# A transformer pair on one core: RMS norms without a scaling step, and pair scores issued ahead of transposes

## The reference, cut to what matters

```python
def rmsnorm(x, g):
    x32 = x.astype(jnp.float32)
    y = x32 * lax.rsqrt(jnp.mean(x32 * x32, axis=-1, keepdims=True) + EPS)
    return (y * g.astype(jnp.float32)).astype(x.dtype)
```

```python
s = einsum('bnqhgd,bnshd->bnhgqs', q, kb) * HEAD_DIM ** -0.5 + bias     # 64-wide heads
s = where(mask, s, -inf)
p = softmax(concatenate([s, sink], axis=-1), axis=-1)[..., :-1]
o = einsum('bnhgqs,bnshd->bnqhgd', p, vb)
return o.reshape(B, S, N_HEADS * HEAD_DIM) @ w_out
```

## Time and profile before

| what | value |
|---|---|
| median of three runs | 2370.95 us |
| profiled execution, its own time | 2369.46 us |
| its span | 2367.7 us |
| TensorE busy | 2346.6 us, 99% |
| VectorE busy | 1437.1 us, 61% |
| ScalarE busy | 1149.5 us, 49% |
| GpSimd busy | 23.9 us, 1% |
| granted TensorE clock, mean | 0.998 |
| HBM traffic | 185 GB/s over the span |

### The profile page before, as it was taken

How to read it: one execution, slowest core, us unless ns; L and a number is a source line. 1 busy time by engine, 2 the same in 40 slices (tenths; PEclk the granted TensorE clock), 3 DMA queues, 4 the chain that set the end, 5 groups by cost and what they waited for, 6 DMA issues and landing times.

```text
span 2367.7 us, 28497 instructions
## 1 busy us (share of the span) xinstructions
PE 2346.6 (99%) x11298; PEld 1963.7 (83%) x11298; DVE 1437.1 (61%) x2039; ACT 1149.5 (49%) x1704; POOL 23.9 (1%) x35
## 2 busy tenths in 40 slices
PE   8999999999999999999999999999999999999998
PEld 7888888888888888888888887788888888888886
DVE  6445565665554454454444566657888888885444
ACT  6445454545444444444444566655544444444442
POOL 1000000000000000000000100000000000000000
PEclk9999999999999999999999999999999999999999
DMA  7666555655666666666666665455666666666564
GB/s 261 187 187 175 156 174 152 186 185 181 195 187 189 193 188 188 193 188 205 191 191 190 209 197 163 131 151 179 188 193 189 189 193 188 189 193 191 192 194 151
DMA packets 226420, 439.25 MB, mean 186 GB/s; under 512 B 13632, under 2 KB 17888, under 8 KB 225904
## 3 DMA queue, kind: packets, MB, share of 16 engines
q1 hardware_dynamic: 224400, 429.51, 60.5%
q0 software_dynamic: 1888, 7.93, 1.1%
HBM read 435.24 MB, written 2.15 MB: 185 GB/s over the span
## 4 chain that ended last, share of the span: by engine, by line
PE 97%; ACT 1%; DVE 1%; issue 0%; DMA 0%; POOL 0%; DVEq 0%; ACTq 0%; POOLq 0%
PE bank L1357 24%; PE bank L1359 24%; PE bank L1358 24%; PE bank L1387 14%; PE bank L1389 7%; PE bank L1399 2%; PE bank L1543 1%; PE bank L1564 1%; PE bank L1442 0%; ACT whi L605 0%; PE bank L1459 0%; PE bank L1540 0%; PE bank L1565 0%; PE bank L1444 0%; ACT JK L597 0%
## 5 line engine op out<-in xcount | busy, mean ns | idle before, releaser
L906 DVE TENSOR_TENSOR wlo<-raw,whi 128x1024 fp32r<-128x1024 f32 (+1 forms) x812 | 988.1, 1218 | 883.3 <-ACT whi L605 882.6
L605 ACT CAST whi<-raw 128x1024 fp32r<-128x1024 f32 (+1 forms) x812 | 847.4, 1044 | 1158.7 <-PE bank L1359 907.0
L1357 PE MATMUL bank<-whi,TT 128*128 128x512 f32 (+1 forms) x1488 | 591.2, 397 | 3.2 <-DVE wlo L906 3.1
L1359 PE MATMUL bank<-whi,TT 128*128 128x512 f32 (+1 forms) x1488 | 578.2, 389 | 0.0
L1358 PE MATMUL bank<-wlo,TT 128*128 128x512 f32 (+1 forms) x1488 | 577.4, 388 | 0.0
L1387 PE MATMUL bank<-TT,whi 128*128 128x512 f32 x1408 | 488.9, 394 | 0.8 <-DVE TT L1147 0.7
L1389 PE MATMUL bank<-TT,wlo 128*128 128x256 f32 x1408 | 390.1, 277 | 0.0
L1357 PEld LDWEIGHTS bank<-whi,TT 128*128 128x128 f32 x1488 | 279.9, 188 | 62.1 <-DVE wlo L906 4.0
L1358 PEld LDWEIGHTS bank<-wlo,TT 128*128 128x128 f32 x1488 | 280.1, 188 | 58.1 <-issue 2.9
L1359 PEld LDWEIGHTS bank<-whi,TT 128*128 128x128 f32 x1488 | 279.6, 188 | 58.1
L1387 PEld LDWEIGHTS bank<-TT,whi 128*128 128x128 f32 x1408 | 264.0, 188 | 62.5 <-issue 1.3
(11 more groups left out here) (211 smaller groups left out, 1586.6 us busy)
## 6 DMA issues: line engine op xcount, KB each, us to landing
raw<-in_ffn_w_up_dram SPq DMA_DIRECT2D x176, 512.0 KB, 3.6
raw<-in_w_in_dram SPq DMA_DIRECT2D x120, 512.0 KB, 3.7
raw<-in_w_gate_dram SPq DMA_DIRECT2D x88, 512.0 KB, 3.7
raw<-in_w_up_dram SPq DMA_DIRECT2D x88, 512.0 KB, 3.7
raw<-in_w_down_dram SPq DMA_DIRECT2D x88, 512.0 KB, 4.7
raw<-in_ffn_w_down_dram SPq DMA_DIRECT2D x88, 512.0 KB, 4.8
raw<-in_swa_w_in_dram SPq DMA_DIRECT2D x48, 512.0 KB, 3.6
raw<-in_w_out_dram SPq DMA_DIRECT2D x32, 512.0 KB, 4.6
```

The source lines that it names most:

```text
L605: eng.copy(whi[:, t % RING, 0:a * n], raw[:, t % RAW, 0:a * n]).then_inc(s_cast, 1)
L906: eng.tensor_tensor(wlo[:, t % RING, 0:a * n], raw[:, t % RAW, 0:a * n], whi[:, t % RING, 0:a * n].bitcast(F32), ALU.subtract).then_inc(s_ ...
L1357: eng.matmul(o, lh[:, ts], hi[:, kk, :], start=start, stop=False)
L1359: mm = eng.matmul(o, ll[:, ts], hi[:, kk, :], start=False, stop=stop)
```

## The change

It has two parts. In the norms, `square` passes scale = width^-0.5 to ScalarE's Square, so each sum is already divided by the width; `SS` has ten columns for a norm instead of eight, filled with EPS by one memset at the start of VectorE's program, and each half (token tile) of a norm owns one more column, which nothing overwrites. `reduce_sum` takes that column in too, and the multiply-add at L1004 goes, with the wait in front of it. ScalarE waits once for the memset. In `side_steps`, wherever a step t has a `pscore`, every `pptr` and `ppcp` of that t is taken out of the list and put back right behind the first `pscore`. By the table of steps this alters four lists: in 511 and 519 the order "ppcp, pptr, pscore" becomes "pscore, ppcp, pptr", and in 512 and 520 "ppcp, psoft, pscore" becomes "psoft, pscore, ppcp". The banks of these steps change with the order.

```diff
@@ side_steps @@
+    for t in range(END):
+        late = [z for z in at[t] if z[0] in ("pptr", "ppcp")]
+        if any(z[0] == "pscore" for z in at[t]):
+            rest = [z for z in at[t] if z not in late]
+            n = rest.index(next(z for z in rest if z[0] == "pscore"))
+            at[t] = rest[:n + 1] + late + rest[n + 1:]
     put(544, "gain", 2)
@@ build @@
-        SS = sb("SS", [P, 9, 8])
+        SS = sb("SS", [P, 9, 10])
@@ square @@
+                n = (SQ[r] - (SQ[r - 1] if r else 0)) // 2
+                col = col // n * (n + 1) + col % n
+                ac.wait_ge(s_eps, 1)
                 if squares[0]:
                     ac.wait_ge(s_sq, squares[0])
                 squares[0] += 1
-                eng.activation(JK[:, 0:src.shape[-1]], src, ACT.Square,
+                eng.activation(JK[:, 0:src.shape[-1]], src, ACT.Square, scale=SQ_WIDTH[r] ** -0.5,
                                accum_out=SS[:, r, col:col + 1]).then_inc(s_sq, 1)
@@ mean_of @@
-                eng.reduce_sum(MEAN[:, r, :], SS[:, r, 0:2 * n].rearrange("p (t n) -> p t n", n=n),
-                               AX).then_inc(s_red, 1)
-                ve.wait_ge(s_red, r + 1)
-                eng.tensor_scalar(MEAN[:, r, :], MEAN[:, r, :], 1.0 / SQ_WIDTH[r], EPS, ALU.mult,
-                                  ALU.add).then_inc(s_mean, 1)
+                eng.reduce_sum(MEAN[:, r, :], SS[:, r, 0:2 * n + 2].rearrange("p (t n) -> p t n", n=n + 1),
+                               AX).then_inc(s_mean, 1)
@@ vector_program @@
+            eng.memset(SS[:, :, :], EPS).then_inc(s_eps, 1)
             first_T(0)
```

More of the change, by code:

```diff
@@ L368, in build @@
         l_lines, l_gf, l_g1, l_g3, l_bt0, l_bt1, l_out = sems("lines gf g1 g3 bt0 bt1 out")
-        s_sq, s_red, s_mean, s_rs, s_rs34, s_mhalf = sems("sq red mean rs rs34 mhalf")
+        s_sq, s_eps, s_mean, s_rs, s_rs34, s_mhalf = sems("sq eps mean rs rs34 mhalf")
         s_pf, s_ang, s_nn, s_sin, s_trig, s_gfn, s_biasmm, s_biasln = sems(
```

## The result

The changed kernel took 2376.72 us in the median of 22 runs (2367.84 to 2378.62), beside 2370.28 us for the kernel before in 22 runs of the same chip (2369.45 to 2371.42). The forecast was 2369.1 us, the range ended at 2371.2, and the median lies 5.5 us above that end.

A forecast was written before the change was run, and what follows sets the result against it. The prediction took TensorE, busy 2346.6 of 2367.7 us, to bound the kernel. The order's 1.27 us plus three norms at 0.19 gave 1.84 less: 2370.95 - 1.84 = 2369.1 us, range 2367.5 to 2371.2.

The forecast's parts named there:

- The order: Steps 511 and 519: TensorE's waits for YL move onto the last two transposes, gaining 0.64 and 0.63, together 1.27 us.
- The norms: Multiply-add dropped from nine norms: three touch the chain and gain 0.19 us each; the other six were taken as nothing.
- norms 6 and 8: Transposes of X after one norm, bare end of program at the other: 0.19 us less each without the multiply-add.
- norm 0: Chain from L1004 through the power and ScalarE back to TensorE: 0.19 us earlier, bounds 0 and 0.27.
- Rival 1: Waits for the PT copy at steps 509 and 517: the 1.27 us return there; 2370.4 us, chance 0.12.
- Rival 2: Waits for YL vanish wholly because what frees the bank also comes sooner; 2367.3 us, chance 0.05.
- Rival 3: ScalarE's squares: the scale costs 87 ns each, shrinking the gain to 0.88 us; 2370.1 us, chance 0.06.
- Rival 4: Steps 513 and 521: psoft ahead of the PT copy delays the product reading PT, 5.7 us; 2374.8 us, chance 0.04.
- What is added: In the norms: memset, one ScalarE wait, two more elements in a reduction, scale in 60 squares; taken as 0, worst 0.96 us.
- The range: Whole kernel: 2367.5 to 2371.2 us, from bounds 2367.3 and 2371.0 and a spread of 0.4 us between runs.
- the chance of 0.95: Whole kernel: time within 0.2%, 4.7 us, of before; 0.02 for a larger gain, 0.03 for a larger loss.
- The last part: Signs to check in the trace; a time outside the range would mean something else moved, such as TensorE's granted clock, 0.998 before.

The follow-up runs named there:

- e2: Kernel before with only the new order of the side steps, norms as before: 2369.12 us in 11 runs, ratio 0.9995.
- e11: Kernel before with only the norms' part, SS allocated behind all other tiles so nothing moves: 2369.36 us in 11 runs, ratio 0.9996.
- e5: Changed kernel with SS allocated behind all other tiles and a dead tile in its old place, so nothing moves: 2368.30 us, ratio 0.9992.
- e10: Changed kernel with SS in its new place and a 32-byte dead tile in front of RA: 2368.22 us in 11 runs, ratio 0.9990.
- e1: Kernel before with only the norms' part, side steps in the old order: 2378.28 us in 6 runs, ratio 1.0034.
- e3: The changed kernel run again with no edit: 2376.97 us in 7 runs, ratio 1.0029 against the kernel before.
- e4: Kernel before with SS at ten columns instead of eight and nothing else changed: 2379.80 us in 5 runs, ratio 1.0033.
- e8: Changed kernel plus one small identity product ahead of the fifth group of wide products: 2377.14 us in 6 runs, ratio 1.0029.
- e12b: Changed kernel plus a small product ahead of the fifth group, 120 columns read 32 bytes further on in ident: 2377.59 us, ratio 1.0027.
- e13b: e5 plus one small identity product ahead of the fifth group of wide products: 2376.11 us in 10 runs, ratio 1.0023.

## Why the prediction was right in its parts and wrong in the time

**The order, right.** Predicted 1.27 us; e2 measured 1.2, with an interval from about 3 us less to 1 more, so it is the trace that bears it out: the waits stand where the prediction put them. The sizes were a little off in ways that cancel. I had the first four transposes begin at 1488.53, 0.11 us behind the start of YL (1488.42), and take 0.44. They begin just there (1489.22, YL at 1489.11) but take 0.60, so TensorE waits 0.21 and 0.72 us instead of 0.38 and 0.88. What follows the wait took 0.44 us where I had 0.49. In the chain, YL's end to the next chunk is 0.04 + 0.44 us in both places, against 0.04 + 1.13 and 1.12 before, so the gain in the trace is 0.69 + 0.68 = 1.37.

**The norms, right in sign, small in size.** Predicted 0.57 us. e11 measured 1.0, and e5 and e10 measured 2.0 and 2.2 for the whole against 1.84; the intervals of e11 and e5 hold 1. In the trace each of norms 6 and 8 shows its 0.19 where it was forecast, and norm 0 0.16, behind a head that came 0.84 later. The other 0.4 us of e11 I can't place: medians of eleven runs with a spread of 2 us don't settle it. The product followed the reduction's start by 0.08 us although the reduction lasts 0.16, as the rows of before had suggested for two independent instructions. The Trainium skill ("VectorE: DVE Perf Modes", "The DRAIN you can't avoid") says that the next operation waits until the pipe is empty, but also that one which is not held starts earlier. The prediction used only the first sentence; the 0.08 us agrees with the second.

**The rivals.** Rival 1: the waits for the PT copy are 0.8 us against 0.7, not 0.6 grown. Rival 2: the waits for YL did not vanish. Rival 3: the squares are as long as before, by

```profile
L606 ACT ACTIVATE JK<-bank 128x512 bf16<-128x512 f32 x12 | 7.1, 595 | 7.9 <-PE bank L1367 7.8
```

595 ns, the number in the earlier trace rows. Rival 4: no wait at the products with V. Its time, 2374.8, comes nearest to the median of all that I wrote, and its mechanism is absent: a near number is no evidence for a cause.

**The step that failed** is "What is added" in part one. It lists the memset, the wait, two more elements and the scale, and takes 0 for them. It priced the instructions of the two extra columns and not their address. The missing term is: SS grows, RA and RB move onto a multiple of 64 bytes, and the row products that read them are the last break ahead of 1360 pairs of products, which then run at 353.3 instead of 346.7 ns: 39 of 52 runs lie in the upper group. The term is 9.0 us when it falls so, nearly five times the forecast gain. Two sizes failed with it. The range took 0.4 us for the spread of one kernel's runs, from three runs, where the 22 of before spread by 2.0. And the chance of 0.95 for a time within 0.2% left 0.03 for a loss of over 4.7 us; the median lies 6.4 above that of before. The 8 of 22 runs at the forecast are those in which the missing term came to nothing. The last part named the granted clock as what might move; it was 0.997 in both groups. The trace of before did hold a sign of it: its first 48 pairs run in all three forms, which the mean of the group of 1408 hides. I had read that group as a constant.

**What stays open.** Shown: the loss sits in the pairs' rate; the rate is kept until something breaks the run of pairs; the place of RA and RB shifts the odds of which rate follows; a break elsewhere can throw it as well. Not shown: how the place acts, and that it acts through the row products' reading of RA and RB, which fits all runs but is argued. The gap between the pairs on either side of the rows differs by a few ns between kernels (717 ns between the starts in before, 715 in e1, e3, e4, e8 and e12b), but e10 has 715 and is fast and the changed kernel's own trace, of the lower group, has 708, so the gap alone does not fix it. A longer or shorter reading of the operands is a guess that I did not test.

## What to carry to other kernels

When a tile grows, allocate it behind all the others, or pad it, so that an edit is timed apart from the tiles that it moves; in a long stage of back-to-back products such a move can outweigh the edit. Look at all runs and not only at the median: two groups with nothing between them point to something that falls one way or the other in each execution, and the means of the groups of products in one run of each show where. If products become slower by a constant few ns each, with no wait and at the same granted clock, look for the last thing that broke their run, and test it by moving that or by adding a break.

## What the hardware showed that I had not expected

A pair of 512- and 256-wide products in a steady stream has more than one stable rate at the full granted clock: 346.7 ns and 353.3 ns, 1.9% apart. One unrelated product of 0.14 us changed it for the next 1152 pairs in the trace of e13b, and all 10 of its runs lie where that puts them. Tiles moved by 32 bytes in a partition took the share of runs in the upper group from 0 of 115 to 8 of 12. And the program's first stretch at the full clock began some 2 us later in the changed kernel's trace than in that of before (the windows above), which left it 0.84 us late; traces with the same norms as before show both forms.
